# A ring of five places for the gathered expert rows, two of them lent by other buffers

## The reference, cut to what matters

```python
def block(xb):                                   # 128 tokens, 8 heads, 16 experts a head
    q = (xb @ w_query).reshape(TOKEN_BLOCK, PEER_HEADS, 2, PEER_QDIM // 2)
    s = jnp.einsum("nhpd,hpkd->nhpk", q, sub_keys)
    ...                                          # top 16 pairs of keys: eidx, gates g
    u = u_tab[eidx]                              # 16384 experts of 2048 channels
    hid = jax.nn.gelu(jnp.einsum("nd,ned->ne", xb, u), approximate=False)
    w = g * hid
    return jnp.einsum("ne,ned->nd", w, v_tab[eidx])
x = x + gate2 * rmsnorm(peer(h))
```

## Time and profile before

| | |
|---|---|
| median of 3 runs | 3299.02 us (3294.02 to 3302.07) |
| the profiled execution, its own time | 3297.2 us |
| its span, first to last instruction | 3295.1 us |
| granted TensorE clock, mean over the span | 0.993 |
| busy share of the span: PE, PEld, DVE, ACT, POOL | 98%, 90%, 82%, 32%, 35% |
| matmuls | 19393 |
| gathers: number, GpSimd idle before those of `u` and of `v` | 342, 747.4 us and 625.6 us |

### The profile page before, as it was taken

One profiled execution on the slowest core, in us unless ns is written; L12 is line 12 of the kernel. 1 busy time (PEld: TensorE's weight loads), 2 busy tenths in 40 slices (PEclk: granted clock), 3 DMA queues, 4 the chain that ended last, 5 costly groups with the idle time before them and its releaser, 6 DMA issues. The chain is left out here.

```text
span 3295.1 us, 48421 instructions
## 1 busy us (share of the span) xinstructions
PE 3225.9 (98%) x19393; PEld 2975.4 (90%) x19393; DVE 2697.7 (82%) x3810; ACT 1053.1 (32%) x1401; POOL 1154.9 (35%) x602
## 2 busy tenths in 40 slices
PE   6999999998999999999999999999999999999998
PEld 3788888888995448999999999999999999999998
DVE  2599999998885669968788888888688888888888
ACT  3223232323222004952323322323322323323332
POOL 2343333332541765013233333334133333233332
PEclk9999999999999999999999999999999999999999
DMA  9745454445557112569899999999799998999887
GB/s 400 282 165 172 157 175 161 167 169 214 196 184 288 64 39 98 226 261 362 337 371 359 355 358 362 353 346 367 291 360 356 357 351 346 361 351 353 341 341 306
DMA packets 174476, 914.55 MB, mean 278 GB/s; under 512 B 16303, under 2 KB 54104, under 8 KB 80088
## 3 DMA queue, kind: packets, MB, share of 16 engines
q1 hardware_dynamic: 125046, 553.37, 45.5%
q0 software_dynamic: 49248, 358.63, 28.0%
HBM read 876.31 MB, written 34.55 MB: 276 GB/s over the span
## 5 line engine op out<-in xcount | busy, mean ns | idle before, releaser
L1441 ACT ACTIVATE sb_raw_hi<-sb_raw_ring 128x2048 fp32r<-128x2048 f32 x256 | 491.0, 1918 | 1144.5 <-DMA sb_raw_ring<-in_v_t 561.3
L1962 DVE TENSOR_TENSOR sb_raw_lo<-sb_raw_ring,sb_raw_hi 128x2048 fp32r<-128x2048 f32 x256 | 585.0, 2285 | 107.1 <-ACT sb_raw_hi L1441 107.0
L1102 PE MATMUL ps_all<-sb_w_hi,sb_raw_hi 128*128 128x342 f32 x2032 | 639.5, 319 | 7.5 <-ACT sb_raw_hi L1441 3.9
L1041 PE MATMUL ps_all<-sb_h_hi,sb_raw_hi 128*128 128x342 f32 x2048 | 646.0, 320 | 0.0
L1041 PE MATMUL ps_all<-sb_h_lo,sb_raw_hi 128*128 128x342 f32 x2048 | 645.6, 320 | 0.0
L1103 PE MATMUL ps_all<-sb_w_lo,sb_raw_hi 128*128 128x342 f32 x2032 | 638.6, 320 | 0.0
L2291 POOL DMA_INDIRECT sb_gather_ring<-in_u_tab,sb_kept x171 | 293.3, 1715 | 747.4 <-DVE sb_kept L2092 571.0
L2291 POOL DMA_INDIRECT sb_gather_ring<-in_v_tab,sb_kept x171 | 298.7, 1747 | 625.6 <-DVE sb_acc_a L2105 425.4
L2195 POOL TENSOR_TENSOR sb_w_low<-sb_w_raw,sb_w_high 128x1536 fp32r<-128x1536 f32 (+1 forms) x63 | 260.0, 4127 | 406.8 <-ACT sb_w_high L1250 406.8
L1102 PEld LDWEIGHTS ps_all<-sb_w_hi,sb_raw_hi 128*128 128x128 f32 x2032 | 384.7, 189 | 10.0 <-ACT sb_raw_hi L1441 5.6
L1041 PEld LDWEIGHTS ps_all<-sb_h_lo,sb_raw_hi 128*128 128x128 f32 x2048 | 386.0, 188 | 0.0
(11 more groups left out here) (311 smaller groups left out, 5367.5 us busy)
## 6 DMA issues: line engine op xcount, KB each, us to landing
sb_raw_ring<-in_u_t SPq DMA_DIRECT2D x128, 1024.0 KB, 7.3
sb_raw_ring<-in_v_t SPq DMA_DIRECT2D x128, 1024.0 KB, 7.7
sb_arena<-in_ada_wt SPq DMA_DIRECT2D x96, 512.0 KB, 4.3
sb_w_raw<-in_w_t SPq DMA_DIRECT2D x32, 1024.0 KB, 5.8
sb_small<-in_ada_w SPq DMA_DIRECT2D x31, 1024.0 KB, 11.3
sb_w_raw<-in_w_v SPq DMA_DIRECT2D x32, 768.0 KB, 4.3
sb_g_ring<-table_scratch SPq DMA_DIRECT2D x32, 684.0 KB, 10.7
table_scratch<-sb_stage SPq DMA_DIRECT2D x8, 2432.0 KB, 8.4
```

Source lines behind the costliest of these rows:

```text
L1041: last = mm(acc, raw_hi[:, r[0], kk * P:(kk + 1) * P], part[:, kk, :], start=i == 0, stop=False)
L1102: mm(accs[c], v, w_hi[:, slots[e], :], start=e == 0, stop=False)
L1441: acti(raw_hi[:, k % 2, :], raw_ring[:, k % RAW, :], ACT.Copy).then_inc(S["un_hi"], 1)
L1962: vec.tensor_tensor(raw_lo[:, k % RAW, :], raw_ring[:, k % RAW, :], raw_hi[:, k % 2, :].bitcast(f32), ALU.subtract)\
```

## The change

The gathers get up to five places (`WIDE`). Gathers 0 to 9 and the last six (336 to 341) use only the three places of `gather_ring`; all others take the place whose last use is oldest. In the pass over `u` places 3 and 4 are `acc_a` and `acc_x`, in the pass over `v` they are `h2a` and `h2x`. The first gather into each borrowed accumulator (gathers 10 and 11) also waits for 15 low parts (`w_lo`), since the accumulators hold kept GELU results; a `v` gather goes into `h2a` or `h2x` only after dot 170. Since these two places are also those of `last_x[0]` and `last_x[1]`, the two residual loads move from k = 137 to k = 251 (`UNITS - 5`) of SP's list, behind a wait for `gr_used` to reach 336. Two semaphores are needed for the new places; the three `rows_in`, `dist_in` and `silu_in` become one, `head_in`, and all who waited for one of them wait for all six transfers.

With this rule gather 10 goes to place 3 and 11 to place 4 (both unused before), 12 to place 1 (last used by 7), 13 to place 2 (by 8), 14 to place 0 (by 9), 15 to place 3 (by 10); 339 goes to the place of 336, 340 to that of 337, 341 to that of 338.

```diff
+WIDE = 5
+def gather_places():
+    places, last = [], [-1] * WIDE
+    for n in range(2 * DOTS):
+        if n == DOTS:
+            last[GRING:] = [DOTS - 1] * (WIDE - GRING)
+        allowed = range(WIDE if 10 <= n < 2 * DOTS - 6 else GRING)
+        place = min(allowed, key=lambda p: last[p])
+        places.append((place, last[place]))
+        last[place] = n
+    return places
+GPLACES = gather_places()
+def gather_use(n):
+    return sum(p == GPLACES[n][0] for p, _ in GPLACES[:n + 1])
...
+        def gather_at(n):
+            place = GPLACES[n][0]
+            if place < GRING:
+                return gather_ring[:, place, :]
+            return ((acc_a, acc_x) if n < DOTS else (h2a, h2x))[place - GRING]
...
-            sp.wait_ge(S["silu_in"], 32)
+            sp.wait_ge(S["head_in"], 96)
...
-                if k == TURN + 3:
-                    sp.wait_ge(S["gr_used"], DOTS)
+                if k == UNITS - 5:
+                    sp.wait_ge(S["gr_used"], 2 * DOTS - 6)
                     for t in range(2):
                         sp.dma_start(last_x[t], x1_d[t * P:(t + 1) * P, :]).then_inc(S["last_in"], 16)
...
-            dve.wait_ge(S["rows_in"], 48)
+            dve.wait_ge(S["head_in"], 96)
...
-            dve.wait_ge(S["dist_in"], 16)
+            dve.wait_ge(S["head_in"], 96)
...
-                wait(dve, f"gr_in{n % GRING}", 16 * (n // GRING + 1))
-                ring = gather_ring[rows, n % GRING, :]
+                wait(dve, f"gr_in{GPLACES[n][0]}", 16 * gather_use(n))
+                ring = gather_at(n)[rows, :]
...
-                wait(pool, "gr_used", n - GRING + 1)
-                pool.indirect_dma_start(out=gather_ring[:, n % GRING, :], ...
+                wait(pool, "gr_used", GPLACES[n][1] + 1)
+                if n < DOTS and GPLACES[n] in ((GRING, -1), (GRING + 1, -1)):
+                    pool.wait_ge(S["w_lo"], EARLY)
+                pool.indirect_dma_start(out=gather_at(n), ...
```

More of the change, by code:

```diff
@@ L351, in bank @@
             return psum[:, i * NB:(i + 1) * NB]
-        names = """consts rows_in dist_in x_in sumsq silu_e silu colsT cols_ev lg_e
-            silu_rows silu_out silu_in col_in0 col_in1 col_in2 col_in3 col_a col_used late_cols late_t late_row late_out bias_in silu_w gate2_cols gate2_t gate2_bias gate2_row gate2_out
+        names = """consts head_in x_in sumsq silu_e silu colsT cols_ev lg_e
+            silu_rows silu_out col_in0 col_in1 col_in2 col_in3 col_a col_used late_cols late_t late_row late_out bias_in silu_w gate2_cols gate2_t gate2_bias gate2_row gate2_out
             ada_in0 ada_in1 ada_in2 ada_in3 ada_in4 ada_done ada_ev row_t mod_b xtr h_tmp h_high h_low
@@ L361, in build_program @@
             x1_out h2x_in xe_in un_in0 un_in1 un_in2 un_hi un_lo un_half un_done g_in0 g_in1 gelu gated w_hi w_lo y_ev
-            gr_in0 gr_in1 gr_in2 gr_used hid_gelu hid_w fin_in last_in last_rest y_last pick_x yt_done sq_done zs y y_out
+            gr_in0 gr_in1 gr_in2 gr_in3 gr_in4 gr_used hid_gelu hid_w fin_in last_in last_rest y_last pick_x yt_done sq_done zs y y_out
             dve pool spare""".split()
@@ L481, in _ @@
             piece_load(0, 3)
-            sp.dma_start(lg_all, decay.partition_broadcast(P)).then_inc(S["rows_in"], 16)
-            sp.dma_start(lam_in, lams.partition_broadcast(P)).then_inc(S["rows_in"], 16)
-            sp.dma_start(iota[:, :], iota_c).then_inc(S["rows_in"], 16)
+            sp.dma_start(lg_all, decay.partition_broadcast(P)).then_inc(S["head_in"], 16)
+            sp.dma_start(lam_in, lams.partition_broadcast(P)).then_inc(S["head_in"], 16)
+            sp.dma_start(iota[:, :], iota_c).then_inc(S["head_in"], 16)
             sp.wait_ge(S["silu_out"], 16)
             sp.wait_ge(S["ada_done"], ADA_PIECES)
-            sp.dma_start(dist, dist_c).then_inc(S["dist_in"], 16)
+            sp.dma_start(dist, dist_c).then_inc(S["head_in"], 16)
             for g in range(GROUPS):
@@ L497, in _ @@
             for g in range(GROUPS):
-                sp.dma_start(silu_b[:, g, :], silu_d[g:g + 1, :].partition_broadcast(P)).then_inc(S["silu_in"], 16)
-            sp.wait_ge(S["silu_in"], 32)
+                sp.dma_start(silu_b[:, g, :], silu_d[g:g + 1, :].partition_broadcast(P)).then_inc(S["head_in"], 16)
+            sp.wait_ge(S["head_in"], 96)
             head_loads(0, first=True)
@@ L2097, in accumulate @@
                 rows = slice(0, P if own else XP)
-                wait(dve, f"gr_in{n % GRING}", 16 * (n // GRING + 1))
-                ring, acc = gather_ring[rows, n % GRING, :], (acc_a if own else acc_x)[rows, :]
+                wait(dve, f"gr_in{GPLACES[n][0]}", 16 * gather_use(n))
+                ring, acc = gather_at(n)[rows, :], (acc_a if own else acc_x)[rows, :]
                 if n - DOTS in (0, 1):
@@ L2263, in _ @@
                 x1_root(t)
-            pool.wait_ge(S["rows_in"], 48)
+            pool.wait_ge(S["head_in"], 96)
             for hd in range(PEER_HEADS):
@@ L2288, in _ @@
                     pool.wait_ge(S["xe_in"], 32 * XG)
-                wait(pool, "gr_used", n - GRING + 1)
-                pool.indirect_dma_start(out=gather_ring[:, n % GRING, :], out_offset=None, in_=u_tab if n < DOTS else v_tab,
+                wait(pool, "gr_used", GPLACES[n][1] + 1)
+                if n < DOTS and GPLACES[n] in ((GRING, -1), (GRING + 1, -1)):
+                    pool.wait_ge(S["w_lo"], EARLY)
+                pool.indirect_dma_start(out=gather_at(n), out_offset=None, in_=u_tab if n < DOTS else v_tab,
                                         in_offset=bass.IndirectOffsetOnAxis(ap=eidx_a[:, c:c + 1] if own else eidx_x[:, c - SLOTS:c - SLOTS + 1], axis=0))\
-                    .then_inc(S[f"gr_in{n % GRING}"], 16)
+                    .then_inc(S[f"gr_in{GPLACES[n][0]}"], 16)
             pool.wait_ge(S["sq_done"], 1)
```

## The result

The changed kernel takes 3312.84 us (median of 5 runs, 3312.49 to 3315.02), the kernel before in the same comparison 3299.02 us (5 runs, 3294.02 to 3304.53). The ratio is 1.0042, interval 1.0027 to 1.0056: 13.8 us slower by the medians, where the forecast was 7.7. The forecast's 3306.7 is 6.1 us too low, and the measured time lies 0.3 us above the range.

The account below looks back on a forecast made before the run. TensorE, busy 1637.72 of 1640.00 us in the long stretch, was taken to bound the kernel. Terms 0 + 5.5 + 0 + 2.2 + 0 = +7.7 us on 3299.0 gave 3306.7 us, range 3299.5 to 3312.5.

Parts of the forecast that it names:

- The deeper ring itself: Five gather places remove at most 24.5 us of VectorE waits, hidden by its free time; at most 2.2 us, taken as 0.
- The hole in round 23: Gather 10 waits for the 15th low part, its dot starts 5.5 us late, and TensorE's unit 25 takes it all: +5.5 us.
- I take 0 for this burst: Behind the wait gathers 10 to 14 leave in close order; they were to land before they are wanted: 0.
- the later weight loads have the same 5.5 us to spare: After the wait in round 23, TensorE asks for each unit 5.5 us later, so weight loads gain that time; burst priced 0.
- The end, +2.2: Residual tiles ahead of unit 255's load make it take 12.4 us instead of 8.5, delaying VectorE's last work: +2.2 us.
- The merged semaphore, 0: At the head VectorE also waits for the SiLU broadcasts, covered by 2.7 us of idle time: 0.
- hole and tail at their larger prices: Rival: gather 10 takes 9.3 us or more to land and the tail costs 2.7 to 4; 3309 to 3314, chance 0.27.
- The hole is covered: Rival: gather 10 lands in 5.4 us and unit 255's load is hidden; +3.5 or less, 3300 to 3303, chance 0.14.
- if the burst of five gathers holds a weight load for more than the hole gives: Sign named at the prediction's end for the sum of +7.7 us being too low; no size given.
- The wait for 336: Rival: accumulate 335 over 4.1 us later makes SP hold back unit 255's loads; 1 for 1 beyond that, chance 0.02.
- the rival in which late gathers hold TensorE unseen: Rival: late gathers hold TensorE through VectorE, so five places remove gaps; 9.9 us needed for over 0.3% faster, chance 0.06.

Follow-up runs that it names:

- Version 3: Changed kernel with accumulators lent from gather 14 instead of 10 and the residual tiles loaded behind unit 255's load: ratio to the kernel before 0.9995, 3301.97 us.
- before: The kernel before the change, with three gather places, and its first profiled execution: 3299.02 us in the comparison of the result.
- number 12: The kernel before, unedited, profiled a second time: that execution's own time was 3305.61 us.
- 4: Kernel before with only the merged semaphore for the head's small loads: ratio 0.9998, 3302.89 us.
- 6: Kernel before with only the two residual tiles moved to k = 251, ahead of unit 255's load: ratio 1.0019, 3309.36 us.
- version 8: Changed kernel with first borrowed place from gather 14, second from gather 24, and residual tiles behind unit 255's load: ratio 0.9998, 3301.82 us.
- version 1: Changed kernel with the two accumulators lent from gather 14 on instead of 10: ratio to the kernel before 1.0008, 3305.60 us.
- after: The changed kernel in its first profiled execution, which took 3315.02 us; median of its runs 3312.84 us, ratio 1.0042.
- 9: The changed kernel itself again, for a second profiled execution: ratio to the kernel before 1.0023, 3312.19 us.
- version 2: Changed kernel with the two residual tiles loaded one step later, behind unit 255's load: ratio to the kernel before 1.0015, 3308.54 us.
- version 5: Kernel before with its three places, but gathers 10 and 11 wait for the 15th low part: ratio 1.0015, 3307.25 us.
- 10: Changed kernel with the first borrowed place from gather 10 and the second only from gather 24: ratio to the kernel before 1.0020, 3308.88 us.
- 11: Kernel before with three places, gathers 10 and 11 waiting for the 15th low part, and residual tiles ahead of unit 255's load: ratio 1.0030, 3312.95 us.
- number 7: Changed kernel with 40 unused matmuls filling TensorE's gap before unit 25: ratio to the kernel before 1.0029, 3311.51 us.
- the second comparison: Changed kernel against the kernel before, measured again: 3312.19 us (10 runs) against 3301.69 us (30 runs), ratio 1.0023.

## Why the forecast was right in its direction and too small

The step that failed is the one that priced the burst at nothing; the profiles show about 2.3 us for it. The sizes of the two large terms held, one of them by luck. Term by term:

- **The deeper ring itself, 0**: right as far as it can be measured. Version 3 is 0.9995; TensorE's waits in the long stretch are 2.2 and 1.2 us, while VectorE's for gathers fell by 18.4 us. The 3 us by which the long stretch is shorter with five places, if they are real, would be a gain that the sum lacks.
- **The hole in round 23, +5.5**: each step as forecast, 7.3 us for the gather, 5.3 of idle VectorE, 6.4 more in unit 25's gap. Two things were not in it. The clock, +2.6 us in the pair of profiles. And, against it, that before usually has a stall of its own there, whose cause the wait partly removes: with gather 10 held back, block 15's load has less beside it (used 7.9 to 10.6 us after its issue in the seven profiles with the wait, 12.2 to 12.8 in the four with the stall). Over the table, from unit 15 to the 20th matmul of unit 25: the seven profiles with round 23 as before (before, 12, 4, 6, 8, 1, 3) average 86.2 us, the six with the wait (after, 9, 2, 5, 10, 11) 91.4. So clock and all, the wait costs 5.2 us, and version 5 measured 5.0 (1.0 to 8.6). The first average hangs on how often before has its stall (82.8 to 83.6 us without, 87.8 to 88.9 with it). The term's size held because two things that it left out cancel, which is luck.
- **"I take 0 for this burst"**: this is the step that failed, and with it the sentence that "the later weight loads have the same 5.5 us to spare". They have nothing to spare, for SyncE is held too. Its list has the load of gate rows ahead of unit 27's load, and the gate rows wait for VectorE's gate of block 15, which the hole makes late. TensorE was done with unit 24 at 1540.26 - 7.33 = 1532.93, so SyncE could have loaded unit 27 5 us sooner. In before the gate rows go at 1526.23 and unit 27's load at 1527.99, 0.94 us ahead of unit 25's first matmul; in after the gate rows wait for the end of the row of 1537.02, and the load goes behind them at 1537.98, 2.28 us ahead of it. Instead of 5.5 us the load gains 1.3, and 2.6 more from the slower matmuls of unit 25. Before it took 14.2 us, with nothing to spare: ScalarE has its high part at 1542.20 + 1.92 = 1544.12, and unit 27 starts at 1544.17. After it could have taken 14.2 + 1.3 + 2.6 = 18.1, and took 19.8: 1.7 us too long, for a gap of 1.56. For behind the wait the load takes longer, the more gathers leave in close order. From issue to ScalarE's use: with three gathers 12.1 and 12.5 us (5, 11), with four 15.7 (10), with five 19.8, 19.9, 20.6 and 19.9 (after, 9, 2, 7). Up to four it is hidden; with five TensorE waits 1.56, 2.50 and 2.28 us (4.24 in number 7, at the full clock), and the stage to unit 27 averages 14.2 us instead of 12.0 in after, 9 and 2: 2.3 us. Without the wait the number of gathers doesn't order the loads so: 13.7 to 16.3 us with three places (before, 12, 4, 6), 17.9 in 8, and with the same six gathers 12.6 in 1 and 22.0 in 3. The 2.3 us are read from the profiles; the run times of 9 and 10 don't resolve them. And no run moves the load of the gate rows, so how much the held list adds and how much the slower load isn't shown. The bandwidth is the likeliest reason for the slower load. The DMA queues, from the load's issue to its use, after and before (packets, MB, share of the engines; q0 carries GpSimd's gathers, q1 SyncE's loads):

```profile
q0 software_dynamic: 778, 5.70, 68.3%
q1 hardware_dynamic: 1407, 2.53, 34.1%
```

```profile
q0 software_dynamic: 452, 3.31, 57.6%
q1 hardware_dynamic: 1384, 2.35, 44.8%
```

  Both windows are full: 8.25 MB in 1538 to 1558 us are 412 GB/s, 5.68 MB in 1528 to 1542 are 406. SyncE's queue moves about the same 2.4 MB in both, but needs 20 us for it instead of 14, while 2.4 MB more of gathers go with it. (The Trainium skill, "DMA: Bandwidth & Descriptors", section "Queues, rings and completion order", has each DMA engine take turns between queues, packet by packet. The trace fits: a gather's packets average 7.3 KB and SyncE's 1.8 KB here, and the gathers get the larger part.)
- **The end, +2.2**: mechanism and load time (12.4 us) as forecast. What it lacked is the clock of the transposes, 1.0 us at the end of the span in the profiles of after and 9 (none in 1 and 10). Over the table's last stretch, the four profiles with three places and unmoved tiles average 83.0 us, the four of the changed end with five places (after, 9, 10, 1) 84.6, or 85.4 with number 7: 1.7 to 2.4 us. With three places it is 88.8 (6, 11), 5.8 us more. With five and the tiles behind 81.7 (2, 3, 8), so that with the ring held the same the tiles cost 2.9 to 3.7 us. The spread within a group is up to 4 us, so these are sizes, not measurements to the microsecond. What lies between 6 and the forecast's 2.2 goes with the load of unit 255, 15.4 us there.
- **The merged semaphore, 0**: right, 0.9998. That the head was 4.5 us longer in the profile of after (175.7 us to the same matmul, 171.1 before) is scatter: number 12 has 174.0 with the old semaphores, version 8 170.8 with the new one.

Together 5.2 + 2.3 + 2.0 = 9.5 us, against 7.6 (4.3 to 11.2) in the second comparison and 13.9 (8.9 to 18.5) in the first. With the 3 us that the long stretch may give back it would be 6 to 7. The missed term is 2.3 us of the 6.1 by which the forecast fell short of the first comparison, which is not explained in full. It has five runs of each kernel, and the median of before is 1.8 to 2.7 us below the three later ones; what else parted them, no run here shows. Of the rivals, "hole and tail at their larger prices" has the right size for the wrong reason: the gather took 7.3 us, not 9.3. "The hole is covered" lost: no gap was less than 5.2 us in any profile with the wait, but for number 7, where matmuls fill it. The remark that the sum is too low "if the burst of five gathers holds a weight load for more than the hole gives" was the one that came true, and it should have had a term. The wait for 336 didn't hold SyncE: the tiles follow unit 254's load within 0.1 us. And the rival in which late gathers hold TensorE unseen isn't shown: version 3, which takes most of their waits away, has an interval that ends at 0.9984, so it gains 5.3 us at most.

No version beats the kernel before. The best, 3 and 8, equal it.

## What to carry to other kernels

A deeper buffer pays where the consumer's wait reaches the engine that bounds the kernel; look there first, for 18 us of waits can go and the time stay. Where the new buffers are borrowed, price the moment of the loan: the gather that can't leave ahead, and then all that leave at once when the lender is done, with the transfers of other queues beside them; with the places brought in one by one, as in 8 and 10, no gap stood behind the burst. And read the slack of a stage from more than one execution: the 0.97 us here were 4.0 to 4.6 in four of seven. Last, when an engine is late, ask what its own waits hold in the list of another: SyncE's late load, together with the gathers beside it, was the cost that had no term.

## What the runs showed of the hardware

- TensorE's clock behind its gaps. The first 12 matmuls of a unit take 1.95 to 2.01 us at the full clock and 3.4 to 3.6 at the lower one. In the fourteen profiles, behind every gap up to 1.6 us they took 1.95 to 2.01 us, behind every gap from 3.94 to 8.8 us ahead of a unit 3.22 to 3.59. In between both happen: 2.28 us was followed by 2.01 (version 2), 1.99 us by 2.75 (number 12), 2.65 us by 1.96 (version 3, unit 15) and 2.72 us by 3.22 (before, the same unit). At the end a gap of 2.83 us (after) was followed by slower transposes, one of 2.88 us (version 1) was not.
- Behind five gathers of 1 MB issued within 7 us of each other, a weight load of 1 MB took 19.8 to 20.6 us, while some 410 GB/s went through the DMA queues; behind three it took 12.1 and 12.5. But two profiles with the same six gathers around it had 12.6 and 22.0 us.
- GpSimd needs 0.94 us to issue a gather in VectorE's hole, and often 2.3 to 2.75 us elsewhere in the same rows. In the profile of before 148 of the 342 issues took over 1.5 us, and VectorE was at work in 147 of them for at least 90% of the first 0.9 us, nearly always with one of its long operations on 2048 columns (L1962, L2092, L2105). No short issue needs an idle VectorE (73 of 194 had it at work), but none of the long ones had it idle. So the hole itself probably let the burst leave faster.
